# Moving conditioning products and loads between stages, splitting the first up-projection, scaling behind the last norm, and filler products on PE

## The reference, cut to what matters

```
for layer in 0, 1:                       # first block
    mod = silu(c) @ ada_w[layer] + ada_b[layer]       # 1024 x 6144, one row
    shift_m, scale_m, gate_m, shift_f, scale_f, gate_f = split(mod, 6)
    h = rmsnorm(x, g) * (1 + scale_m) + shift_m
    x = x + gate_m * mixer(h)            # layer 0: convolution and retention; layer 1: S5 and GLU
    h = rmsnorm(x, g) * (1 + scale_f) + shift_f
    x = x + gate_f * (relu(h @ w_fc1[layer])**2 @ w_fc2[layer])    # 4096 wide
x = rmsnorm(x, norm_f)
h = rmsnorm(x, g_mix)                    # second block: three attention branches
x = x + (gated sum of three branches of h @ w_in) @ w_out
h2 = rmsnorm(x, g_ffn)
return x + (silu(h2 @ w_ffn_gate) * (h2 @ w_ffn_up)) @ w_ffn_down  # 2816 wide
```

## Time and profile before

| | us |
|---|---|
| median of 3 runs (1374.43 to 1382.37) | 1379.83 |
| profiled execution | 1379.8 |
| its span | 1378.0 |
| PE busy (products), PE busy (weight loads) | 1242.6, 1139.7 |
| DVE, ACT, POOL busy | 795.6, 502.3, 370.9 |
| mean granted clock of PE | 0.958 of full |

### The profile page before, as it was taken

How to read it: one execution, slowest core, us unless ns; L and a number is a source line. 1 busy time by engine, 2 the same in 40 slices (tenths; PEclk the granted TensorE clock), 3 DMA queues, 4 the chain that set the end, 5 groups by cost and what they waited for, 6 DMA issues and landing times.

```text
span 1378.0 us, 23730 instructions
## 1 busy us (share of the span) xinstructions
PE 1242.6 (90%) x10368; PEld 1139.7 (83%) x10368; DVE 795.6 (58%) x913; ACT 502.3 (36%) x654; POOL 370.9 (27%) x581
## 2 busy tenths in 40 slices
PE   1699998889989986889899999997989998899999
PEld 1587587778879966879799999796769998799998
DVE  4896886334463437964586533647765465555353
ACT  2221122111113433433555432446457743444341
POOL 7999653555414806920000000000000021000000
PEclk9899999999999998989999999998989999999999
DMA  8964666988774474406355445343332453355451
GB/s 322 362 216 155 227 213 225 333 285 301 284 289 161 154 259 160 155 21 244 122 172 182 184 183 181 131 146 109 123 122 92 154 184 123 123 184 184 157 210 62
DMA packets 118791, 258.14 MB, mean 187 GB/s; under 512 B 5056, under 2 KB 18656, under 8 KB 118560
## 3 DMA queue, kind: packets, MB, share of 16 engines
q1 hardware_dynamic: 86160, 185.78, 38.3%
q10 hardware_dynamic: 27584, 51.01, 10.1%
q0 software_dynamic: 4944, 19.83, 4.0%
HBM read 241.93 MB, written 14.68 MB: 186 GB/s over the span
## 4 chain that ended last, share of the span: by engine, by line
PE 67%; DVE 13%; DMA 9%; ACT 4%; issue 3%; POOL 3%; DVEq 0%; POOLq 0%; ACTq 0%
PE bank L1737 67%; DMA ada_slot<-in_ada_w 6%; DVE ada_acc L1233 4%; DVE big L1330 3%; POOL big L747 2%; DVE rstd L1243 1%; DMA memory_kv<-s_tables 1%; POOL big L740 1%; DVE ring_split L1281 1%; ACT ada_slot_split L831 1%; DMA ring<-in_w_ffn_down 1%; DVE h_in L1264 1%; DMA ring<-in_w_glu_a 1%; DMA ring<-in_w_ffn_up 1%; DVE ada_acc L1230 0%
## 5 line engine op out<-in xcount | busy, mean ns | idle before, releaser
L1737 PE MATMUL bank<-squares_split,ring_split 128*128 128x256 f32 x800 | 227.2, 284 | 0.0
L1737 PE MATMUL bank<-h_in,ring 128*128 128x256 f32 x832 | 197.6, 399 | 7.3 <-ACT h_in L792 7.2
L1737 PEld LDWEIGHTS bank<-h_in,ring 128*128 128x128 f32 x832 | 165.4, 201 | 32.8 <-issue 7.5
L753 POOL TENSOR_TENSOR y_cat<-y_cat,tmp 128x512 f32<-128x512 f32 x8 | 10.7, 1343 | 537.5 <-DVE tmp L1669 537.5
L1737 PEld LDWEIGHTS bank<-squares_split,ring_split 128*128 128x128 f32 x800 | 154.3, 193 | 0.0
L1233 DVE SCALAR_TENSOR_TENSOR ada_acc<-ada_slot,cact,ada_acc 128x512 f32<-128x512 f32 x168 | 133.9, 797 | 6.0
L1737 PE MATMUL bank<-ada_slot_split,ring_split 128*128 128x256 f32 x432 | 122.3, 283 | 0.0
L1737 PE MATMUL bank<-h_in_split,ada_slot_split 128*128 128x256 f32 x384 | 111.7, 291 | 8.0 <-DVE y_cat_split L1673 3.8
L1281 DVE TENSOR_TENSOR ring_split<-ring,ada_slot_split 128x2048 fp32r<-128x2048 f32 (+1 forms) x32 | 72.2, 2257 | 80.0 <-ACT ada_slot_split L831 80.0
L1737 PE MATMUL bank<-big_split,ring_split 128*128 128x256 f32 x352 | 100.3, 285 | 0.0
L831 ACT ACTIVATE ada_slot_split<-ring 128x2048 fp32r<-128x2048 f32 (+1 forms) x32 | 60.2, 1885 | 70.6 <-PE bank L1737 42.6
(11 more groups left out here) (409 smaller groups left out, 3565.2 us busy)
## 6 DMA issues: line engine op xcount, KB each, us to landing
ring<-in_w_fc SPq DMA_DIRECT2D x32, 2048.0 KB, 8.5
ada_slot<-in_ada_w ACTq DMA_DIRECT2D x22, 2048.0 KB, 12.6
ring<-in_w_in SPq DMA_DIRECT2D x19, 2048.0 KB, 7.9
ring<-in_w_ffn_gate SPq DMA_DIRECT2D x5, 2048.0 KB, 7.7
ring<-in_w_ffn_up SPq DMA_DIRECT2D x5, 2048.0 KB, 8.1
ring<-in_w_ffn_down SPq DMA_DIRECT2D x5, 2048.0 KB, 8.0
ring<-in_w_out SPq DMA_DIRECT2D x4, 2048.0 KB, 9.4
ring<-in_w_branch SPq DMA_DIRECT2D x3, 2048.0 KB, 7.7
```

What stands on the lines that cost most here:

```text
L753: pool.tensor_tensor(merged, merged, tmp3[:, 2 * p:2 * p + 2, :], ALU.add).then_inc(s("mga"), 1)
L1737: return pe.matmul(*args, skip_group_check=True, **kw)
```

## The change

- **Loads.** The first four pieces of `ada_w` are issued on SP's queue right behind x, without waits, into four places (both buffers, the end of `big`, the third ring buffer); the constants move from POOL's queue to SP's, behind the second panel. Piece 4 follows on ACT's queue when the first panel has landed.
- **First conditioning.** For `ada0` to `ada3` DVE takes six slabs; PE takes two with silu(c) as a one-column operand. `ms0` moves in front of `ada0`, its reciprocal behind `ada_acc(1)`.
- **Convolution.** DVE does the taps of both halves in a row and then adds PE's taps, so `cv0`'s bank is freed after both; `ada5` and `ada6` move behind the rotation.
- **First up-projection.** `f1.0` becomes split products, with 16 more units and `norm(1)` split.
- **Spread.** Of `ada10` to `ada21` six stay in `f1.0` (DVE in halves), six go to `f2.0`, `ada22` and `ada23` to `f1.1`. `wt1` to `wt4` stand behind `f1.0.1`, `.5`, `.9`, `.13`, `wt5` to `wt7` in blocks 0, 2 and 4.
- **Branches.** `fk0`, `nr0`, `nr1`, `fk1` move in front of `cs0`; `nr4` and `nr5` one and two rounds later on all engines.
- **Last norm.** The last feed-forward takes x times its gain without the reciprocal root; `ms6` follows `fg0`, and DVE multiplies each `fg` and each silu by it (22 more instructions of 128x512). The low parts of the merged branches start earlier.
- **Filler.** `keep_busy` issues 4 or 6 products of constants, 384 columns each, in front of `f1.0.0`, `uu0`, `ga0` and `ms3`.

```diff
-SW_ADA = 2
+EARLY_ADA = 4
+KEEP_BUSY = {"f1.0.0": 4, "uu0": 6, "ga0": 4, "ms3": 6}
+DVE_SLABS = 6
-ADA_AFTER = {1: 10, 2: 11, 3: 12, 5: 13, 6: 14, 7: 15, 9: 16, 10: 17, 11: 18, 13: 19, 14: 20, 15: 21}
+ADA_AFTER = {3: 10, 6: 11, 8: 12, 11: 13, 13: 14, 15: 15}
+ADA_LOAD_AFTER = {2: 12, 5: 13, 7: 14, 10: 15, 12: 16, 14: 17}
+ADA_HALVES = {0: (10, 0), 1: (10, 1), 2: (11, 0), 4: (11, 1), 5: (12, 0), 6: (12, 1), 7: (13, 0), 9: (13, 1),
+              10: (14, 0), 11: (14, 1), 12: (15, 0), 13: (15, 1)}
+S5_AFTER = {1: 1, 5: 2, 9: 3, 13: 4}
+SIDE_ADA = {0: 16, 1: 17, 3: 18, 4: 19, 5: 20, 6: 21}
+SIDE_S5 = {0: 5, 2: 6, 4: 7}
...
-        SPLIT_NORMS = (3, 5, 6)
+        SPLIT_NORMS = (1, 3, 5, 6)
-        freed.update({"cv0": ("cvadd", 1), "cv1": ("cvadd", 3)})
+        freed.update({"cv0": ("cvadd", 1), "cv1": ("cvadd", 2)})
...
             sp.dma_start(x, a["x"].rearrange("(k p) t -> p k t", p=P)).then_inc(s("x_in"), 16)
+            for k in range(EARLY_ADA):
+                sp.dma_start(ada_slot(k), ada_source(k)).then_inc(ada_in(k)[0], 16)
...
             ada_mod(4)
-            ada_acc(5)
...
+            convolve(1, 0, DVE_TAPS)
+            add_taps(0)
...
-            for k in range(10, 23):
-                ada_acc(k)
-                if k > 10:
-                    ada_mod(k - 1)
+            for j in range(16):
+                if j + 3 < FC:
+                    split_low(j + 3)
+                if j in ADA_AFTER and j < 15:
+                    ada_mod(ADA_AFTER[j])
+                if j in ADA_HALVES:
+                    k, half = ADA_HALVES[j]
+                    ada_acc(k, 4 * half, 4 * half + 4)
+            ada_acc(16)
+            ada_mod(15)
...
+            def keep_busy(name):
+
+                for _ in range(KEEP_BUSY[name]):
+                    mm(ps(name)[:, 0:3 * P], inv1024, inv[:, :], start=True, stop=True)
...
-            for i in range(8):
-                w = panel(f"f1.0.{i}")
-                for j in range(2 * i, 2 * i + 2):
-                    project(f"f1.0.{j}", w, 2 * (j % 2), h, h_ready(1) if j == 0 else no_wait)
+            for j in range(16):
+                project_split(f"f1.0.{j}", j, *input_parts(1), input_ready(1) if j == 0 else no_wait)
...
-            mean_squares(6)
             for u, name in enumerate(last_jobs):
                 project_split(name, LAST + u, *input_parts(6), input_ready(6) if u == 0 else no_wait)
+                if u == 0:
+                    mean_squares(6)
```

More of the change, by code:

```diff
@@ L91, in job_order @@
     jobs += ["ga0", "ga1", "gb0", "gb1", "ga2", "ga3", "gb2", "gb3", "ms3", "mk0", "mk1"]
[L92 removed]
+    jobs += ["f1.1.0", "mkr0", "f1.1.1", "mkr1"]
+    for j in range(2, 16):
+        jobs.append(f"f1.1.{j}")
+        if j in (5, 9):
+            jobs.append(f"ada{22 + j // 9}")
     jobs += [f"f2.1.{p}" for p in range(4)] + ["ms4", "mv0", "ms5", "mv1"]
[L94 to L95 removed]
+    jobs += ["gq0", "gk0", "ff", "gv0", "gv1", "la", "gg0", "gg1", "fq0", "fq1", "fk0", "kot",
+             "nr0", "nr1", "fk1", "cs0", "cs1", "at0", "at1", "go0", "gor0", "nr2", "nr3", "go1", "gor1",
              "fv0", "fv1", "mq0", "mq1"]
@@ L102, in job_order @@
         bg += 1
-        if u == 0:
-            jobs += ["nr4", "nr5"]
+        if u in (1, 2):
+            jobs.append(f"nr{3 + u}")
         if 1 <= u <= 8:
@@ L109, in job_order @@
     jobs += ["bg10", "bg11"]
-    jobs += [f"br{i}.{p}" for i in range(3) for p in range(4)] + [f"w2o.{p}" for p in range(4)] + ["ms6"]
-    for p in range(6):
+    jobs += [f"br{i}.{p}" for i in range(3) for p in range(4)] + [f"w2o.{p}" for p in range(4)] + ["fg0", "ms6", "fg1", "fu0", "fu1"]
+    for p in range(1, 6):
         n = 2 if p < 5 else 1
@@ L374, in add_units, with buffers_at @@
                     units.append((name, c0, width, buffers[(len(units) - base) % 3]))
+        def buffers_at(places):
+            return [split[name][:, o:o + 2048] for name, o in places]
         base = 0
         FC2 = 2
+        T_, B_, Y_ = buffers_at((("tmp", 0), ("big", 6144), ("y_cat", 0)))
+        for i in range(16):
+            units.append((f"f1.0.{i // 2}", 256 * (i % 2), 256, ((T_, B_, Y_) * 4 + (T_, Y_) * 2)[i]))
+        base = FC = len(units)
         add_units([f"f2.0.{b}" for b in range(FC2, 8)], 512, [split[name][:, 0:2048] for name in ("h_in", "y_cat", "tmp")])
@@ L1146, in _ @@
                 split_high(LAST + u)
-            squares(6)
             for k in range(KT):
-                input_high(6, k)
+                act.wait_ge(s("xres"), 33 + k)
+                act.activation(input_parts(6)[0][:, k, :], x[:, k, :], ACT.Copy, scale=col("g_ffn", k)).then_inc(s("h_high"), 1)
+            for c in range(4):
+                act.activation(yt3[:, 2 * c:2 * c + 2, :], x[:, 2 * c:2 * c + 2, :], ACT.Square).then_inc(s("sq"), 1)
+            root("ms6")
             for u, name in enumerate(last_jobs):
@@ L1227, in ada_acc @@
                     dve.wait_ge(s("cact"), 1)
-                for i in range(KT):
+                for i in range(first, min(end, n)):
                     if i == 0:
@@ L1287, in act_low, with low6, residual @@
                 tt(big_lo[:, m:m + 2, :], big3[:, m:m + 2, :], big_hi(m, 2).bitcast(F32), ALU.subtract).then_inc(s("a_low"), 1)
-            def residual(r, name, gate):
+            def low6(k):
+                dve.wait_ge(s("h_high"), 8 * SPLIT_NORMS.index(6) + k + 1)
+                high, low = input_parts(6)
+                stt(low[:, k, :], x[:, k, :], col("g_ffn", k), high[:, k, :].bitcast(F32), ALU.mult, ALU.subtract).then_inc(s("h_low"), 1)
+            def residual(r, name, gate, after=None):
                 for p in range(4):
+                    if after and p:
+                        after(2 * p - 2)
+                        after(2 * p - 1)
                     job_wait(dve, f"{name}.{p}")
@@ L1821, in ada @@
                 begin(f"ada{k}")
+                early_slabs = range(DVE_SLABS, KT) if k < EARLY_ADA else ()
+                if early_slabs:
+                    pe.wait_ge(s("cact"), 1)
+                    pe.wait_ge(*ada_in(k))
+                for slab in early_slabs:
+                    for i in range(4):
+                        mm(ps(f"ada{k}")[:, i:i + 1], ada_slot(k)[:, slab, P * i:P * i + P], cact[:, slab:slab + 1],
+                           start=(i == 0 and slab == DVE_SLABS), stop=False)
                 pe.wait_ge(s("ada_acc"), k + 1)
                 for i in range(4):
-                    last = mm(ps(f"ada{k}")[:, i:i + 1], accb[:, 512 * (k % 2) + P * i:512 * (k % 2) + P * i + P], one[:, :], start=(i == 0), stop=(i == 3))
+                    last = mm(ps(f"ada{k}")[:, i:i + 1], accb[:, 512 * (k % 2) + P * i:512 * (k % 2) + P * i + P], one[:, :],
+                              start=(i == 0 and not early_slabs), stop=(i == 3))
                 end(last)
@@ L2161, in _ @@
                 end(last)
-            for j in range(2):
-                project_split(f"fk{j}", PROJ + 8 + j, *h2, no_wait)
             def gla_out(j):
```

317 lines of the change are left out of this document (187 added, 130 removed).

## The result

| | before | after |
|---|---|---|
| median, us | 1378.41 (4 runs, 1374.43 to 1382.37) | 1357.84 (4 runs, 1356.12 to 1358.06) |
| span of the profiled execution | 1378.0 | 1356.3 |
| PE busy (products) | 1242.6 | 1238.4 |
| DVE, ACT, POOL busy | 795.6, 502.3, 370.9 | 844.7, 534.5, 404.5 |
| granted clock of PE | 0.958 | 0.951 |

The account below looks back on a forecast made before the run. PE is full from 700 us on, so gains must come from the start, `f1.0` (waits for `mod`) and later single waits. 8 + 28.5 - 13 + 3.7 + 5.4 - 3.6 + 4.5 + 4.5 = 38 us, giving 1342; range 1306 to 1364.

Parts of the forecast that it names:

- start, to the end of `f1.0.0`: Kernel start: earlier loads let scaling begin at 35, `av0` at 36.3; `f1.0.0` ends at 229.4 instead of 237.4, gain 8.
- `f1.0` behind its first job: Rest of the first up-projection: 102.1 us of work plus waits for POOL and cold returns, 123 instead of 151.6; gain 28.5.
- `f2.0`: Stage after `f1.0`: more sums and waits for POOL at `kl5`, `kl6`, `kl7`; loss 13, between 1 and 19.
- `f2.0`'s end to `v0`: Before the S5 stage: pieces 22 and 23 no longer hold the third table's load, 12 us earlier; gain 3.7.
- S5 stage: The S5 stage itself, forecast 0; the prediction's sum has no separate term for it.
- fillers at `ga0`, `ms3`: Filler products in the waits before these two: gain 2.9 at `ms3` and 2.5 at `ga0`, together 5.4.
- `f1.1`, `f2.1`: `f1.1` gets two sums and 16 products, and DVE falls about 2 us behind with the key norms; loss 3.6.
- branches: Loss 4.5 from a later masked copy, gain 9 from moving `nr4`, `nr5`; together +4.5, between -4.5 and +9.
- `w2o`, last norm, last feed-forward: End of kernel: the 3.78 wait before `w2o` shrinks to about 2, `fg0` starts earlier, `ms6` follows; net gain 4.5.
- The first rival: POOL keeps up, a round in `f1.0` near 25 us, so waits and cold returns go: 1309, between 1306 and 1330; 25%.
- the transfers as a limit: Sign in `f1.0`: transfers over 0.95 busy and DVE waiting for pieces would mean loads are the limit, not POOL.
- the rule's full length: DVE/POOL port lock: blocking for the DVE instruction's whole length would cost 0.3 us more per split, 7 over all rounds.

Follow-up runs that it names:

- (7): Changed kernel with DVE_SLABS = 7, so DVE takes seven slabs and PE one of each of the first four conditioning pieces; 1359.03 us in one run.
- Experiment 5: Changed kernel with DVE working out the S5 scalars ahead of conditioning piece 4 instead of behind it; 1347.5 us.
- Experiment 6: Changed kernel with S5 scalars ahead of piece 4 and PE's taps for the convolution's first half added amid DVE's second half; 1339.97 us, median of three executions.
- the last kernel: Changed kernel with plain `f1.0`, scalars, taps, residual and head norms moved earlier, and S5 blocks behind every third `f1.0` job and `f2.0` blocks 0, 2; 1314.39 us.
- Experiment 8: Changed kernel with DVE adding the first three output-projection residuals before `ada9`'s sum and the first unit's low part; 1349.53 us.
- experiment 2: Changed kernel where ACT and DVE still make all `f1.0` high and low parts, but PE does one plain product of the low parts; 1357.9 us.
- Experiment 1: Changed kernel with plain f32 products in `f1.0` and no splits there or in its norm, rest of the new order kept; 1342.49 us.
- Experiment 9: Two edits of the changed kernel: DVE does two query head norms ahead of the chunk states, 1349.33 us; another has no filler products, 1359.4 us.

## Why the prediction was right or wrong, point by point

| step | forecast | measured (gain, us) |
|---|---|---|
| start, to the end of `f1.0.0` | +8 | -2.4 |
| `f1.0` behind its first job | +28.5 | +29 |
| `f2.0` | -13 | -8.6 |
| `f2.0`'s end to `v0` | +3.7 | +4.3 |
| S5 stage | 0 | -2.9 |
| fillers at `ga0`, `ms3` | +5.4 | +2.1 |
| `f1.1`, `f2.1` | -3.6 | -1.8 |
| branches | +4.5 | -2.0 |
| `w2o`, last norm, last feed-forward | +4.5 | +3.7 |

**The time is in the range and 16 us above the 1342 of the sum.** `f1.0` came out as forecast and `f2.0` cost 4 us less; the start and the branches gave 10 and 6.5 us less than forecast. Up to 4 of the 10 can be the spread of the start between executions, since `f1.0.0` begins at 225.5 to 229.8 in kernels with the same code ahead of it.

**The start failed, by 10 us, at three steps.** (a) The norm's scaling begins at 41.05 instead of 35. Some 2 of the 6 us are piece 3, which landed at 30.0 instead of 27 to 28. For the rest the sum took the slabs on DVE and the sum on PE as one chain. It left out that PE's slabs of piece k wait for `mod(k-1)`, and it priced no product of one column at the lower level: 16 records take 3.57 us. Shifting a slab doesn't help (7). (b) Piece 4 lands at 54.3, not 44.5: it was issued at 35.42 into transfers that were full, behind two panels and the constants, and DVE sat idle for 9.95 us in front of it. Experiment 5 takes that idle time away: 8 us at `f1.0.0` and 8.7 at the first retention product. (c) `cv0`'s bank is the step that was right in kind; `rot3` waits 15.2 us instead of 11, and 6.55 with (b) out of the way. Experiment 6 is its price, 6.6 us by the trace of the last kernel. (d) That the low part of unit 0 delays the first residual was seen and priced at 2.3 us. It was a wait of 3.71 (before: 1.05) and products of 9.65 us (before: 8.70), 3.6 us more than before, because `ada_mod(9)`, a wait for PE until 208.19, stands in the same place. Experiment 8, which takes away the old wait too, gives 5.5 us or more.

**f1.0 was right in size, and right in its mechanism.** Rounds 2, 3 and 4 of POOL took 33.5, 26.9 and 30.3 us from first step to last, 30.2 in the mean; with the 0.9 for issue and hand-over that the forecast counted this is 31.1, and 31.0 was forecast. One by one they differ by what stood beside them: five low parts and 16 conditioning products, three and 9, four and 15, where four and 12 were forecast for each. So the waits at `kl2`, `kl3` and `kl4` were 9.17, 0.44 and 1.77 us instead of 6.1, 5 and 5, 11.4 in all instead of 16. That the stage still took 122.3 us of the forecast 123 is in part luck: a wait of 2.65 us for DVE at `ada14` wasn't in the sum, and two jobs take 11.61 us instead of 11.46. The price of a low part, 1.9 to 2.1 us, was right: beside eight of them in experiment 2 POOL's steps take 1.9 to 2.5 us longer, 2.1 in the mean. That of a conditioning product was a little low: the rounds of the plain `f1.0` take 20.6 to 21.1 us with seven or eight products beside them, 2.8 to 3.3 more than the 17.8 that I estimate for them free (from their steps that nothing stood beside), so 0.4 each and not 0.3. The rows of the waits, `kl2`, `kl3`, `kl4` and then `ada14` for DVE:

```profile
282.65 1.08 PE L1840 MATMUL bank<-prep 128*32 128x64 f32 x32 [9.17 <-POOL prep L715]
313.49 0.65 PE L1840 MATMUL bank<-prep,memory_kv 128*32 128x64 f32 x32 [0.44 <-POOL prep L715]
346.44 1.08 PE L1840 MATMUL bank<-prep 128*32 128x64 f32 x32 [1.77 <-POOL prep L715]
341.97 1.02 PE L1840 MATMUL bank<-one,ada_acc 128*128 128x1 f32 x8 [2.65 <-DVE ada_acc L1286]
```

The first rival (POOL keeps up) is out by the waits themselves, the transfers as a limit by a share of 0.76.

What the prediction did not ask is where its gain came from. It subtracted 15 x 1.42 us for the split and added 21 for the waits behind it, and both were about right; so the split was never a gain, and all of the 29 us belonged to the rest of the new order. Experiment 1 shows it: the new order with plain products gives 33 us in the stage. Of these 16.5 are the waits for `mod`, 4.9 are six sums that moved to other stages, and the other 11.6 are shorter products. How much of it the spread pieces give and how much the moved S5 blocks wasn't tested apart. **The prediction priced the stage as a whole, and priced it right; the kernel that it should have compared with was the change without its costliest part.**

**f2.0** was forecast too dark. `kl5` waits for nothing and `kl6` 1.24 us; round 5 had two plain blocks beside it and took 21.4 us instead of 30. `kl7` waits 4.87 (7.5).

**The branches failed** at the DVE queue. Forecast were a loss of 4.5 at the masked copy and a gain of 9 behind it. The first came true: from the end of `fq1` to the start of `fv0` it takes 3.9 us more, with waits of 4.02 in front of `at1` and 6.43 in front of `go0`. Behind it 3.5 us had come back when the job behind `us4` ended, since the two moved norms now make PE wait 2.29 us in front of `us4`, and 1.9 by `w2o`, behind another wait of 1.27. Experiment 9 repairs the first part.

**The fillers** were priced as if each wait cost its slow start. Only `ms3` is such a place. **The end** was right within 1 us: `w2o` +2.2, `fg0` and `ms6` -0.7, the rest +2.2. **The S5 stage** has a wait called "issue" of 1.75 us and a slow return near 551; waits of 0.7 to 1.8 us of this name stand near that place in ten of the eleven other changed kernels that have a trace as well, and not in the kernel before. They weren't tested, and what causes them stays open.

**The Trainium skill's lock** ("SBUF — State Buffer", section "SBUF: two separate sides") agrees with experiment 2: a DVE instruction with two operands in SBUF holds POOL up. The prediction held the trace against the rule's full length and found it 0.3 us short. In the rows above it isn't: the low part ends at 260.13, POOL's pair at 260.93, 0.8 behind it, which is the pair's own free length, and POOL lost 2.23 us where a low part alone takes 2.29. The smallest losses, 1.88 us in experiment 2, are of steps that began 0.2 us behind the low part.

## What to carry to other kernels

When a part of a change makes the bound engine's work shorter and you expect a new wait because of it, set the two against each other and price the change without that part; here the split of `f1.0` bought some 20 us of PE's time for as much in waits and slow starts, and leaving it out was worth 15 us. Before DVE's work is put beside POOL's, set the length of POOL's round with it against the distance between the points that wait for it: 33 us against 25 is a wait with a slow start, 21 against 24 is none. In an in-order queue look for small work behind a long wait: three swaps of two or three lines on DVE (scalars, residual, head norms) gave 5 to 9 us each by the traces.

## What the runs showed of the hardware

- DVE's low parts (128x2048, two inputs in SBUF) and POOL's steps hold each other up: a pair of steps took 2.99 us instead of 0.76 beside one, and the low part took 2.75 us instead of 2.29. ACT's copies of the same size didn't touch POOL (0.76).
- The effect of DVE on POOL reaches small operations too: in the kernel with plain `f1.0`, a pair of POOL steps took 1.66 us instead of 0.76 where only conditioning products ran on DVE.
- Products of one column take twice as long at the lower level: 8 records take 0.95 us at full clock (151.79 in after) and 1.84 at a granted clock of 0.50 (33.23), 16 records 3.57 there.
- The transfers moved 392 GB/s in the second slice of 34 us, and a transfer issued into it at 35.4 us took 18.8 us to land, where the median of such transfers is 11.9.
- Six filler products with a wait of 0.93 us behind them left `ms3` at the upper level (3.72 us for 16 records, 5.92 without them and with a wait of 4.89). Four in front of `f1.0.0`, with 2.20 us of wait and a slow feed behind them, didn't: the granted clock was 0.67 in the first 10 us of the stage.
